# A block's opening: modulation columns in two channel halves, and the context loaded last

## Chip, cores and metric
The kernel runs on one core of one Trainium2 chip. The metric is device time in microseconds of one execution. Five engines work beside each other: TensorE (PE; PEld is its weight loads), VectorE (DVE), ScalarE (ACT), GpSimd (POOL) and SyncE (SP), which issues the loads. Each runs its own instructions in order and waits on semaphores.

## What is computed
Two stacked networks over 512 tokens of width 1024, in fp32. Only the start of the first matters here:

```python
mod_l = silu(c) @ w_mod + b_mod            # sh1, sc1, g1, sh2, sc2, g2: 6 parts of 1024
mod_c = silu(c_ctx) @ w_mod + b_mod        # the same for the context
pl = (rmsnorm(x, norm1_w) * (1 + sc1) + sh1) @ w_in         # 512 tokens
pc = (rmsnorm(ctx, norm1_w) * (1 + sc1c) + sh1c) @ w_in     # 256 context tokens
ml = mlstm(conv(pl), conv(pc)); hg = hgrn(pl, pc)           # then w_out, a convolved FFN, a second network
```

The opening needs sh1 and sc1 (2048 columns of w_mod) for c and c_ctx, the root of the mean square of each token, and the first slab of w_in.

## The kernel before
**Tiles.** x lies as 8 channel blocks (KD) of 128 channels by 512 tokens, the context cx as 8 by 256. A token tile is used as a sum of two fp32r parts: hh (high) and hl (low) for x, ch and cl for the context. Weights come in slabs of 256 columns (SLAB), all 8 channel blocks of them, and are split in the same way by GpSimd from raw into whi and wlo, in two buffers. A product is three matmuls: high by high, high by low, low by high. Slabs of w_in come in the order of IN1: slab 0 is "mq" (its output is then convolved), slab 1 "mv", slabs 2 and 3 the gates, slab 4 "mq" again.

**The opening** (first() on each engine). SP issues constants, x, cx, eight loads modraw[k] of 1024 KB (channel block k of w_mod, its first 2048 columns), then w_first (slab 0) into raw[0], all on one queue (L643 to L650). ACT squares x and then cx (L1040), DVE adds them up (L2052), PE sums over the partitions with a matrix of ones (square_sum, L3213), ACT takes the root by Ln and Exp (L1043, L1045), and DVE multiplies (L2058): xn for x, cx in place. PE makes the modulation (modulation, L2946): for each k four matmuls of 32 columns of silc (silu of c and c_ctx, the rest zero), by 512 columns of modraw[k], each into its own 32 partitions of pm[1][:, 0, :]. Group g holds columns 512g to 512g + 511, so 0 and 1 are sh1 and 2 and 3 are sc1. ACT copies the 128x512 result to modrow[0] (L1047); mod_turn (L2954) turns it into columns by four small products with the identity; DVE adds the bias and makes modc and wsc (L2064 to L2068), releasing mod_done. Matmuls of idle() (L3209) compute nothing that is used; they fill PE's waits.

**Tokens.** With wsc and modc ACT makes hh[k] (L1054) and for odd k a full-precision copy in pa[3] (L1058); DVE makes that copy for even k (L2078) and takes hl[k] as the difference (L2083). Both go through x's eight blocks and then the context's.

**Slabs.** Slab 0 is slab_opening: for each k six matmuls, as soon as the pieces of its weights (split_first on POOL, FIRST_PIECES) and hh[k], hl[k] are there. Slab 1 is slab_tok_late: clearing matmuls (L2864), then for four tiles of 128 tokens the products of whi (L2868), then those of wlo (L2872), then, once hl_done has counted all sixteen parts, the context's products (L2889 to L2891). Slab 0's result in pm[0] is read by ACT's centre copies (L1085) and by 16 tap operations of DVE (L1781), which then release pm_free[0]. On both engines they stand behind the context's parts. Slab 2 writes pm[0] again and waits for pm_free[0]; its first product is L2641. Loads of later slabs wait for splits, and splits for PE (slab_used).

Of the kernel before, what the change touches and what calls it, by code (L numbers as in the profile page):

```python
# [12 lines left out]
P = 128  # L13
# [37 lines left out]
MOD_GROUP = (0, 0, 0, 0, 1, 1, 2, 3)  # L51
# [24 lines left out]
DIAG_SLOT = (None, None, 8, 10)  # L76

# [95 lines left out]
def build(nc, io):  # L173
    with ExitStack() as ctx:
# [22 lines left out]
        modraw = [place(f"modraw{k}", [P, MOD_W], F32, arena + (12 + 4 * k) * TILE if k < 7 else raw_at - 8 * TILE) for k in range(KD)]  # L197
# [85 lines left out]
        def over_h(name, shape, n, dt=F32):  # L283
# [94 lines left out]
        mod_loaded, mod_used, mod_in, mod_done, lb_step, lb_exp = (  # L378
            [sem(f"mod_loaded{k}") for k in range(KD // 2)], sem("mod_used"), sem("mod_in"), sem("mod_done"), sem("lb_step"), sem("lb_exp"))
# [251 lines left out]
        def _(sp):  # L631
# [13 lines left out]
            sp.dma_start(cx[:].rearrange("p k t -> p (k t)"), io["ctxT"]).then_inc(ctx_loaded, 16)  # L645

            wm = io["w_mod"][0].rearrange("(k p) n -> k p n", p=P)
            for k in range(KD):
                sp.dma_start(modraw[k][:], wm[k][:, 0:MOD_W]).then_inc(mod_loaded[MOD_GROUP[k]], 16)
            sp.dma_start(raw[0][:].rearrange("p k n -> p (k n)"), io["w_first"]).then_inc(raw_loaded[0], 16)  # L650

            for i, (name, c0) in enumerate(IN1):
                if i == 0:
                    continue
                if i == 1:
                    sp.wait_ge(raw_loaded[0], 16)
                if i == 2:
# [353 lines left out]
        def _(act):  # L1011
            act.wait_ge(const_loaded, 16 * 2)
            act.wait_ge(const_made, 3)
            nc.scalar.activation(silc[:, :, 0:2], cols("c", 0, 16).rearrange("p (k j) -> p k j", j=2), ACT.Silu).then_inc(mod_in, 1)
# [17 lines left out]
            def first():  # L1032
                nc.scalar.preload_act_table_set("natural_log_exp_and_others")
                for n, (src, loaded, w) in enumerate(((x, x_loaded, T), (cx, ctx_loaded, CT))):
# [6 lines left out]
                for n, (acc, w) in enumerate(((std, T), (rstd, CT))):  # L1041
# [4 lines left out]
                act.wait_ge(mod_used, KD)  # L1046
                nc.scalar.activation(modrow[0][:], pm[1][:, 0, :], ACT.Copy).then_inc(mod_row, 1)  # L1047
                act.wait_ge(mod_done, 3)
                for n, (src, hi, w) in enumerate(((xn, hh, T), (cx, ch, CT))):
                    act.wait_ge(xn_done, KD * n + KD)  # L1050
                    if n:
                        act.wait_ge(hn_done, KD // 2)
                    for k in range(KD):
                        nc.scalar.activation(hi[:, k, :], src[:, k, :], ACT.Identity, bias=mod_col(0, k, n), scale=wsc[:, n, k:k + 1]).then_inc(hh_done, 1)  # L1054
                        if k % 2:
                            if KD * n + k >= 2:
                                act.wait_ge(hl_done, KD * n + k - 1)
                            nc.scalar.activation(pa[3][:, 0:w], src[:, k, :], ACT.Identity, bias=mod_col(0, k, n), scale=wsc[:, n, k:k + 1]).then_inc(xn_done, 1)  # L1058
# [677 lines left out]
        def _(v):  # L1736
# [306 lines left out]
            def first():  # L2043
                lower_bounds()

                for n, (acc, w) in enumerate(((std, T), (rstd, CT))):
# [8 lines left out]
                for n, (src, dst, w) in enumerate(((x, xn, T), (cx, cx, CT))):  # L2055
                    v.wait_ge(rstd_done, n + 1)
                    for k in range(KD):
                        nc.vector.tensor_tensor(dst[:, k, :], src[:, k, :], pa[n][:, 0:w], ALU.mult).then_inc(xn_done, 1)  # L2058

                v.wait_ge(mod_turned, 1)  # L2060
                to, bias = mod_turned_to(0)
                turned = mod_columns(pm[1][:, 1, :])
                raised = pm[1][:, 1, 4 * MOD_TILES1:5 * MOD_TILES1]
                nc.vector.tensor_tensor(raised.rearrange("p (j g t) -> p t g j", g=2, t=4), turned[:, :, 2:4, :], bias[:, :, 2:4, :], ALU.add).then_inc(mod_done, 1)  # L2064
                nc.vector.tensor_tensor(to[:, :, 0:2, :], turned[:, :, 0:2, :], bias[:, :, 0:2, :], ALU.add).then_inc(mod_done, 1)
                v.wait_ge(mod_done, 2)
                gain = cols("norm1", 0, KD).rearrange("p (o k) -> p o k", o=1).to_broadcast([P, 2, KD])
                nc.vector.scalar_tensor_tensor(wsc[:, 0:2, :], raised.rearrange("p (j k) -> p j k", j=2), 1.0, gain, ALU.add, ALU.mult).then_inc(mod_done, 1)  # L2068
                v.wait_ge(mod_done, 3)
                v.sem_inc(pm_free[1], 1)  # L2070
                for n, (src, hi, lo, w) in enumerate(((xn, hh, hl, T), (cx, ch, cl, CT))):
                    v.wait_ge(xn_done, KD * n + KD)
                    for k in range(KD):
# [6 lines left out]
                        else:  # L2080
                            v.wait_ge(xn_done, 2 * KD + KD // 2 * n + k // 2 + 1)
# [564 lines left out]
        def _(pe):  # L2646
            pe.wait_ge(const_loaded, 16 * 2)
            pe.wait_ge(const_made, 4)
# [29 lines left out]
            def slab_opening():  # L2678

                for k in range(KD):  # L2680
# [180 lines left out]
            def slab_tok_late(b, use, lo):  # L2861
# [32 lines left out]
            def in1(i, between=None):  # L2894
# [16 lines left out]
                elif name in ("mv", "hv"):  # L2911
                    if i == 1:
                        slab_tok_late(b, p, 2 + i + 1)
                    else:
                        slab_tok(b, p)
                    if between:
                        between()
                    pe.wait_ge(hl_done, 2 * KD)
                    last = context_tok(b, p)
                else:  # L2920
                    if i == 0:
                        last = slab_opening()
# [9 lines left out]
            def modulation(first_, end):  # L2932

                for i in range(first_, end):
                    k = i % KD
                    if i < KD:
                        pe.wait_ge(mod_loaded[MOD_GROUP[k]], 16 * MOD_GROUP.count(MOD_GROUP[k]))
                        src, out = modraw[k][:], pm[1][:, 0, :]
                    else:
                        b = mod_buffer(i)  # L2940
                        pe.wait_ge(mod_loaded[b], 16 * (MOD_GROUP.count(b) + sum(mod_buffer(j) == b for j in range(KD, i + 1))))
# [264 lines left out]
            def first():  # L3206
# [343 lines left out]
```

## Time and profile before

| | us |
|---|---|
| median of 3 runs (lowest, highest) | 3009.11 (3007.6, 3009.39) |
| the profiled execution | 3008.7 |
| its span in the trace | 3006.9 |
| PE busy | 2977.1 |
| POOL busy | 2075.4 |
| DVE busy | 1657.6 |
| ACT busy | 1048.0 |

The page gives for each engine the time in which it had an instruction under way. "Idle before" is time in which an engine waited, with the work that released it. Matmuls are pipelined, so the duration of one is longer than the distance of two that follow each other: 389 ns against 0.23 us for the common fp32r product of 512 columns. An fp32 matmul appears as two instructions, one for each pass. PEclk is the share of its full clock that was granted to PE. In the chain of waits and the timeline a row is start, length, and what ran; merged rows carry a count.

### The profile page before, as it was taken

Reading aid. Unit: us, or ns where it says so; the run is one execution under the profiler, and the core shown is the slowest. Engines: PE = TensorE matmul, PEld = TensorE weight load, DVE = VectorE, ACT = ScalarE, POOL = GpSimd, SP = SyncE. Lnnn points to the kernel's source line nnn. Section 1 sums busy time; section 2 is a strip of 40 time slices with the busy share of each in tenths; the row PEclk is TensorE's granted clock in tenths of the full one; section 3 lists DMA queues with packets and bytes.
Section 4 is the critical chain, followed back from the end, with each engine's and each line's share of the span. In section 5 each row is a group of like instructions: output and inputs, shape, how many; then the busy total and the mean of one; then the engine's idle time right before and its main releaser. Section 6 shows DMA issues by size and latency. Waiting matters only on the chain.

```text
span 3006.9 us, 49161 instructions
## 1 busy us (share of the span) xinstructions
PE 2977.1 (99%) x17179; PEld 2584.9 (86%) x17179; DVE 1657.6 (55%) x2214; ACT 1048.0 (35%) x1846; POOL 2075.4 (69%) x1583
## 2 busy tenths in 40 slices
PE   7999999999999999999999999999999999999999
PEld 5878978888889988887889998899888878899987
DVE  5753365889178742364347662577523652477631
ACT  4362153121146620232017650366301320166600
POOL 3614575888778887654777887788876546778874
PEclk9999999999999999999999999999999999999999
DMA  5202262322333333331223333333334313333332
GB/s 222 88 29 63 73 236 71 99 98 80 96 99 103 112 89 107 116 106 64 90 98 99 104 97 96 100 107 102 95 96 136 99 56 98 98 99 98 107 90 83
DMA packets 323100, 300.60 MB, mean 100 GB/s; under 512 B 6652, under 2 KB 316924, under 8 KB 319264
## 3 DMA queue, kind: packets, MB, share of 16 engines
q1 hardware_dynamic: 319056, 290.55, 30.5%
q10 hardware_dynamic: 3920, 8.36, 1.0%
q8 instruction: 82, 1.34, 0.2%
q14 instruction: 42, 0.34, 0.0%
HBM read 292.60 MB, written 2.10 MB: 98 GB/s over the span
## 4 chain that ended last, share of the span: by engine, by line
PE 96%; DVE 1%; DMA 1%; ACT 1%; issue 1%; SPq 0%; DVEq 0%; ACTq 0%
PE pm L2641 16%; PE pm L2643 16%; PE pm L2642 16%; PE pm L2770 8%; PE pm L2771 8%; PE pm L2772 8%; PE pa L2641 2%; PE pa L2643 2%; PE pa L2642 2%; PE pm L2720 1%; PE pm L2721 1%; PE pm L2722 1%; PE pm L3041 1%; DMA modraw<-in_w_mod 1%; PE pm L2671 1%; PE pa L3084 1%
## 5 line engine op out<-in xcount | busy, mean ns | idle before, releaser
L776 POOL TENSOR_TENSOR wlo<-raw,whi 128x512 fp32r<-128x512 f32 (+1 forms) x784 | 977.2, 1278 | 16.4
L772 POOL TENSOR_SCALAR whi<-raw 128x2048 fp32r<-128x2048 f32 (+1 forms) x196 | 336.5, 1717 | 699.8 <-PE pm L2643 326.5
L2641 PE MATMUL pm<-hh,whi 128*128 128x512 f32 x1064 | 421.2, 396 | 2.2 <-DVE sil L2408 2.2
L2643 PE MATMUL pm<-hh,wlo 128*128 128x512 f32 x1064 | 414.3, 389 | 0.0
L2642 PE MATMUL pm<-hl,whi 128*128 128x512 f32 x1064 | 414.3, 389 | 0.0
L794 POOL TENSOR_TENSOR wlo<-raw,whi 128x512 fp32r<-128x512 f32 x216 | 288.2, 1335 | 58.6 <-ACT whi L1445 41.1
L2770 PE MATMUL pm<-tsets,whi 128*128 128x256 f32 x1152 | 326.0, 283 | 0.0
L2771 PE MATMUL pm<-tsets,whi 128*128 128x256 f32 x1152 | 326.0, 283 | 0.0
L2772 PE MATMUL pm<-tsets,wlo 128*128 128x256 f32 x1152 | 326.0, 283 | 0.0
L2641 PE MATMUL pm<-uh,whi 128*128 128x512 f32 x836 | 325.4, 389 | 0.0
L2642 PE MATMUL pm<-ul,whi 128*128 128x512 f32 x836 | 325.2, 389 | 0.0
L2643 PE MATMUL pm<-uh,wlo 128*128 128x512 f32 x836 | 325.2, 389 | 0.0
L2770 PE MATMUL pm<-hh,whi 128*128 128x256 f32 x864 | 244.8, 283 | 0.1
L2771 PE MATMUL pm<-hl,whi 128*128 128x256 f32 x864 | 244.5, 283 | 0.0
L2772 PE MATMUL pm<-hh,wlo 128*128 128x256 f32 x864 | 244.5, 283 | 0.0
L2641 PEld LDWEIGHTS pm<-hh,whi 128*128 128x128 f32 x1064 | 199.8, 188 | 46.8 <-issue 5.7
L2642 PEld LDWEIGHTS pm<-hl,whi 128*128 128x128 f32 x1064 | 199.8, 188 | 43.7 <-issue 3.1
L2643 PEld LDWEIGHTS pm<-hh,wlo 128*128 128x128 f32 x1064 | 199.7, 188 | 42.0
L2356 DVE SCALAR_TENSOR_TENSOR x<-pm,x 128x512 f32 (+1 forms) x32 | 22.1, 692 | 374.4 <-PE pm L2643 374.4
L2770 PEld LDWEIGHTS pm<-tsets,whi 128*128 128x128 f32 x1152 | 221.2, 192 | 0.0
L2771 PEld LDWEIGHTS pm<-tsets,whi 128*128 128x128 f32 x1152 | 221.2, 192 | 0.0
L2772 PEld LDWEIGHTS pm<-tsets,wlo 128*128 128x128 f32 x1152 | 221.2, 192 | 0.0
(549 smaller groups left out, 6755.0 us busy)
## 6 DMA issues: line engine op xcount, KB each, us to landing
raw<-in_w_ffn SPq DMA_DIRECT2D x88, 1024.0 KB, 5.3
raw<-in_w_in SPq DMA_DIRECT2D x61, 1024.0 KB, 5.1
raw<-in_w_ffn SPq DMA_DIRECT2D x64, 704.0 KB, 4.6
raw<-in_w_up SPq DMA_DIRECT2D x22, 1024.0 KB, 5.1
raw<-in_w_out SPq DMA_DIRECT2D x12, 1024.0 KB, 5.1
raw<-in_w_down SPq DMA_DIRECT2D x16, 704.0 KB, 4.6
modbuf<-in_w_mod SPq DMA_DIRECT2D x10, 1024.0 KB, 5.6
modraw<-in_w_mod SPq DMA_DIRECT2D x8, 1024.0 KB, 19.7
```

Of the source, the lines that this page charges most:

```text
L772: nc.gpsimd.tensor_scalar(h, r, 1.0, 1.0, ALU.mult, ALU.mult).then_inc(hi_done, 1)
L776: last = nc.gpsimd.tensor_tensor(o[:, c], r[:, c], h[:, c].bitcast(F32), ALU.subtract)
L794: nc.gpsimd.tensor_tensor(operand(wlo, o), src, operand(whi, o).bitcast(F32), ALU.subtract).then_inc(st_pool, 1)
L2641: nc.tensor.matmul(out, wh, ah, start=start, stop=False)
L2642: nc.tensor.matmul(out, wh, al, start=False, stop=False)
L2643: return nc.tensor.matmul(out, wl, ah, start=False, stop=stop)
L2671: nc.tensor.matmul(pm[use][:, i, :], whi[b][:, k, P * i:P * i + P], src[:, k, :], start=k == 0 and src is hh, stop=False)
L2720: nc.tensor.matmul(o, hh[:, k, c], whi[b][:, k, :], start=k == 0, stop=False)
L2721: nc.tensor.matmul(o, hl[:, k, c], whi[b][:, k, :], start=False, stop=False)
L2770: nc.tensor.matmul(out, wh[:, k, :], th, start=start and k == 0, stop=False, skip_group_check=True)
L2771: nc.tensor.matmul(out, wh[:, k, :], tl, start=False, stop=False, skip_group_check=True)
L2772: last = nc.tensor.matmul(out, wl[:, k, :], th, start=False, stop=k == KD // 2 - 1, skip_group_check=True)
```

## The change
- **Two channel halves.** Each modraw[k] is loaded by two transfers of 512 KB: first the columns of channels 0 to 511 of sh1 and sc1 (groups 0 and 2), for all k, then those of channels 512 to 1023 (groups 1 and 3). PE makes the first half (modulation_half), ACT copies it as two blocks of 32 rows, half_turn turns it, DVE makes four of the eight columns of modc and wsc, and ACT and DVE make hh and hl of k 0 to 3. PE runs slab 0 for these k, then the second half's products, its turn, and slab 0 for k 4 to 7. modrow[0] is cleared at the start, since each turn reads all its rows.
- **w_first in two loads**, channel blocks 0 to 3 ahead of the last two pieces of the first half, and 4 to 7 behind the second half. split_first waits for each.
- **The context last.** cx is loaded behind all of these. Its squares, root, normalization and parts follow x's parts on ACT and DVE; its square_sum is a hook in slab 1, after the second of four token tiles.
- SP no longer waits for w_first before it issues slab 1. modraw[7] lies over whi[1] instead of in hl. full_made takes over one use of xn_done.

```diff
-MOD_GROUP = (0, 0, 0, 0, 1, 1, 2, 3)
+MOD_GROUP = (0, 0, 0, 0, 0, 0, 1, 1, 2, 2, 2, 2, 2, 2, 3, 3)
+FIRST_GROUP, FIRST_K = 1, 4
...
@@ SP @@
+            def mod_columns_of(half, k):
+
+                for_half = [a.rearrange("p (e h c) -> p h e c", e=2, h=2)[:, half] for a in (modraw[k][:], wm[k][:, 0:MOD_W])]
+                sp.dma_start(*for_half).then_inc(mod_loaded[MOD_GROUP[KD * half + k]], 16)
+
+            first_w = raw[0][:].rearrange("p k n -> p (k n)")
+            for k in range(KD):
+                if k == KD - 2:
+                    sp.dma_start(first_w[:, 0:FIRST_K * SLAB], io["w_first"][:, 0:FIRST_K * SLAB]).then_inc(mod_loaded[FIRST_GROUP], 16)
+                mod_columns_of(0, k)
+            for k in range(KD):
+                mod_columns_of(1, k)
+            sp.dma_start(first_w[:, FIRST_K * SLAB:], io["w_first"][:, FIRST_K * SLAB:]).then_inc(raw_loaded[0], 16)
             sp.dma_start(cx[:].rearrange("p k t -> p (k t)"), io["ctxT"]).then_inc(ctx_loaded, 16)
-
-            wm = io["w_mod"][0].rearrange("(k p) n -> k p n", p=P)
-            for k in range(KD):
-                sp.dma_start(modraw[k][:], wm[k][:, 0:MOD_W]).then_inc(mod_loaded[MOD_GROUP[k]], 16)
-            sp.dma_start(raw[0][:].rearrange("p k n -> p (k n)"), io["w_first"]).then_inc(raw_loaded[0], 16)
...
-                if i == 1:
-                    sp.wait_ge(raw_loaded[0], 16)
...
@@ POOL @@
+            nc.gpsimd.memset(modrow[0][:], 0.0).then_inc(const_made, 1)
...
-                pool.wait_ge(raw_loaded[0], 16)
+                pool.wait_ge(mod_loaded[FIRST_GROUP], mod_arrivals(FIRST_GROUP))
                 for i, (k0, k1) in enumerate(FIRST_PIECES):
+                    if k0 == FIRST_K:
+                        pool.wait_ge(raw_loaded[0], 16)
...
@@ ACT @@
+                squares(0)
+                roots(0)
+                act.wait_ge(mod_step, 2)
+                for g in (0, 2):
+                    rows = slice(32 * g, 32 * g + 32)
+                    nc.scalar.activation(modrow[0][rows, :], pm[1][rows, 0, :], ACT.Copy).then_inc(mod_step, 1)
+                act.wait_ge(mod_done, 3)
+                highs(0, 0, FIRST_K)
+                act.wait_ge(mod_used, KD)
+                for g in (1, 3):
+                    rows = slice(32 * g, 32 * g + 32)
+                    nc.scalar.activation(modrow[0][rows, :], pm[1][rows, 0, :], ACT.Copy).then_inc(mod_step if g == 1 else mod_row, 1)
+                act.wait_ge(mod_done, 6)
+                highs(0, FIRST_K, KD)
+                squares(1)
+                roots(1)
+                act.wait_ge(hn_done, KD // 2)
+                highs(1, 0, KD)
...
@@ DVE @@
+                square_sums(0)
+                normalized(0, 0, FIRST_K)
+                v.wait_ge(mod_step, 5)
+                mod_columns_made(0)
+                lows(0, 0, FIRST_K)
+                normalized(0, FIRST_K, KD)
+                v.wait_ge(mod_turned, 1)
+                mod_columns_made(1)
+                v.sem_inc(pm_free[1], 1)
+                lows(0, FIRST_K, KD)
+                square_sums(1)
+                normalized(1, 0, KD)
+                lows(1, 0, KD)
                 v.sem_inc(hn_done, KD)
                 mlstm()
...
@@ PE @@
+                    if between and t == 1:
+                        between()
...
-                    for g in range(4):
+                    for g in range(4) if i >= KD else (1, 3):
                         last = nc.tensor.matmul(out[32 * g:32 * g + 32, :], silc[:, k, :], src[:, T * g:T * g + T], start=k == 0, stop=k == KD - 1)
...
+            def modulation_half():
+
+                for k in range(KD):
+                    pe.wait_ge(mod_loaded[MOD_GROUP[k]], mod_arrivals(MOD_GROUP[k]))
+                    for g in (0, 2):
+                        last = nc.tensor.matmul(pm[1][32 * g:32 * g + 32, 0, :], silc[:, k, :], modraw[k][:, T * g:T * g + T], start=k == 0, stop=k == KD - 1)
+                last.then_inc(mod_step, 1)
+
+            def half_turn(half, bank, done):
+
+                which = ident[:].rearrange("p (g c) -> p g c", g=4)[:, half::2, 0:2]
+                for t in range(4):
+                    last = nc.tensor.matmul(bank[:, 8 * t:8 * t + 8].rearrange("p (g j) -> p g j", g=4)[:, half::2, :], modrow[0][:, P * t:P * t + P], which, start=True, stop=True)
+                last.then_inc(done, 1)
...
                 square_sum(0, std, T)
                 idle(8)
-                pe.wait_ge(mod_in, 1)
-                for k, _ in enumerate(modulation(0, KD)):
-                    if k == 3:
-                        square_sum(1, rstd, CT)
-                    if k == 6:
-                        idle(4)
+                pe.wait_ge(mod_step, 1)
+                modulation_half()
+                idle(4)
+                pe.wait_ge(mod_step, 4)
+                half_turn(0, pm[1][:, 1, :], mod_step)
+                idle(5)
+                slab_opening(0, FIRST_K)
+                for _ in modulation(0, KD):
+                    pass
+                pe.wait_ge(mod_step, 6)
                 pe.wait_ge(mod_row, 1)
-                mod_turn(modrow[0], pm[1][:, 1, :])
-                idle(5)
+                half_turn(1, pm[1][:, 1, :], mod_turned)
                 for i in range(4):
-                    in1(i)
+                    in1(i, (lambda: square_sum(1, rstd, CT)) if i == 1 else None)
```

## Rows read from the trace of the kernel before

**Rows 1.** The page, busy time of the engines.
```profile
PE 2977.1 (99%) x17179; PEld 2584.9 (86%) x17179; DVE 1657.6 (55%) x2214; ACT 1048.0 (35%) x1846; POOL 2075.4 (69%) x1583
```

**Rows 2.** Waits of PE, whole run: us in total, times, longest.
```profile
PE pa L3213 <- DVE std L2052: 18.1, 1, 18.1
PE pm L2641 <- DVE sil L2408: 2.2, 2, 1.1
```

**Rows 3.** The chain that ended last, in the opening: start, us, what.
```profile
34.79 0.61 ACT modrow L1047
...
37.99 1.19 PE pm L2685 x2
```

**Rows 4.** Timeline of PE, opening: start, us, instruction [idle before <-releaser].
```profile
19.93 3.62 PE L3209 MATMUL pm<-ident 128*128 128x128 f32 x16
...
27.58 0.70 PE L3213 MATMUL pa<-rstd,ones 128*128 128x256 f32 x2
...
33.66 1.07 PE L2946 MATMUL pm<-modraw,silc 128*32 128x512 f32 x8 [0.33 <-DMA modraw<-in_w_mod]
```

**Rows 5.** Timeline of PE, slab 1 and the start of slab 2.
```profile
51.21 0.38 PE L2868 MATMUL pm<-whi,hh 128*128 128x256 f32 x1
...
62.81 0.28 PE L2889 MATMUL pa<-whi,ch 128*128 128x256 f32 x1
...
68.57 0.40 PE L2641 MATMUL pm<-hh,whi 128*128 128x512 f32 x1
```

**Rows 6.** Timeline of DVE, opening and slabs 0 and 1.
```profile
18.26 3.60 DVE L2052 TENSOR_TENSOR rstd<-rstd,sq 128x256 f32<-128x256 f32 x7
...
29.24 2.74 DVE L2058 TENSOR_TENSOR cx<-cx,pa 128x256 f32<-128x256 f32 x8 [2.60 <-ACT pa L1045]
...
40.71 1.36 DVE L2083 TENSOR_TENSOR hl<-pa,hh 128x512 fp32r<-128x512 f32 x2
...
46.22 0.54 DVE L2078 TENSOR_SCALAR pa<-cx,wsc,modc 128x256 f32<-128x256 f32 x1
...
52.15 9.73 DVE L1781 SCALAR_TENSOR_TENSOR cacc<-pm,col,cacc 128x441 f32<-128x441 f32 x16 [0.19 <-ACT cacc L1085]
```

**Rows 7.** Windows: PE, PEld, DVE, ACT, POOL busy; PEclk, DMA share, GB/s.
```profile
12.00:23.70 11.70, 5.46 (x18) 4.17 (x18) 10.24 (x20) 8.05 (x17) 0.00 (x0) 1.00 1.01 428
23.70:33.70 10.00, 8.60 (x70) 2.93 (x73) 5.68 (x13) 0.86 (x2) 0.00 (x0) 1.00 1.01 418
37.90:41.30 3.40, 3.31 (x8) 2.69 (x9) 2.77 (x5) 3.40 (x6) 3.23 (x5) 0.50 1.01 338
41.30:50.70 9.40, 9.40 (x43) 7.47 (x42) 8.97 (x18) 9.40 (x18) 8.95 (x9) 1.00 0.11 30
78.00:3006.00 2928.00, 2919.78 (x16824) 2539.68 (x16822) 1616.66 (x2130) 1013.00 (x1788) 2049.81 (x1546) 1.00 0.31 97
```

**Rows 8.** Timeline of all engines: SP's issues of w_mod, ACT's first squares.
```profile
2.63 6.89 SPq L649 DMA_DIRECT2D modraw<-in_w_mod  x8
...
11.28 4.27 ACT L1040 ACTIVATE sq<-x 128x512 f32<-128x512 f32 x8 [4.34 <-DMA x<-in_xT]
```

**Rows 9.** fp32 products of 512 columns (ns, min/median/max), and two modulation weight loads.
```profile
L2946 PE MATMUL pm<-modraw,silc x64: 592/592/826, 23.8 to 34.1; 128*32 128x512 f32 x64
...
L2988 PE MATMUL pa<-mq,mk x48: 590/592/697, 157.3 to 222.7; 128*128 128x512 f32 x48
...
24.46 0.14 PEld L2946 LDWEIGHTS pm<-modraw,silc 128*32 128x32 f32 x4 [0.45 <-issue]
24.89 0.14 PEld L2946 LDWEIGHTS pm<-modraw,silc 128*32 128x32 f32 x4 [0.29 <-issue]
```

**Rows 10.** Timeline of PE, slab 0's third channel block and slab 1's first matmul.
```profile
42.40 0.62 PE L2685 MATMUL pm<-hh,whi 128*128 128x512 f32 x2
...
50.67 0.60 PE L2864 MATMUL pm<-zrow 1*128 1x512 bf16 x2
```

**Rows 11.** Loads by kind: count, size, median us from issue to landing.
```profile
raw<-in_w_gate SPq DMA_DIRECT2D x2, 256.0 KB, 2.7
```

More of the change, by code:

```diff
@@ L196, in build @@
         TILE = 4 * T
-        modraw = [place(f"modraw{k}", [P, MOD_W], F32, arena + (12 + 4 * k) * TILE if k < 7 else raw_at - 8 * TILE) for k in range(KD)]
+        modraw = [place(f"modraw{k}", [P, MOD_W], F32, arena + (12 + 4 * k) * TILE if k < 7 else raw_at + 12 * TILE) for k in range(KD)]
         uh = place("uh", [P, KF, T], F32R)
@@ L377, in build @@
         mod_row, mod_turned = sem("mod_row"), sem("mod_turned")
-        mod_loaded, mod_used, mod_in, mod_done, lb_step, lb_exp = (
-            [sem(f"mod_loaded{k}") for k in range(KD // 2)], sem("mod_used"), sem("mod_in"), sem("mod_done"), sem("lb_step"), sem("lb_exp"))
+        full_made = sem("full_made")
+        mod_loaded, mod_used, mod_step, mod_done, lb_step, lb_exp = (
+            [sem(f"mod_loaded{k}") for k in range(KD // 2)], sem("mod_used"), sem("mod_step"), sem("mod_done"), sem("lb_step"), sem("lb_exp"))
         ctx_free = [sem("ctx_free0"), sem("ctx_free1")]
@@ L1033, in first, with squares @@
                 nc.scalar.preload_act_table_set("natural_log_exp_and_others")
-                for n, (src, loaded, w) in enumerate(((x, x_loaded, T), (cx, ctx_loaded, CT))):
+                def squares(n):
+                    src, loaded, w = ((x, x_loaded, T), (cx, ctx_loaded, CT))[n]
                     act.wait_ge(loaded, 16)
@@ L1040, in first, with roots @@
                         nc.scalar.activation(sqs[m % 4][:, 0:w], src[:, k, :], ACT.Square).then_inc(sq_done, 1)
-                for n, (acc, w) in enumerate(((std, T), (rstd, CT))):
+                def roots(n):
+                    acc, w = ((std, T), (rstd, CT))[n]
                     act.wait_ge(sq_summed, n + 1)
@@ L1045, in first, with highs @@
                     nc.scalar.activation(pa[n][:, 0:w], acc[:, 0:w], ACT.Exp, scale=-0.5).then_inc(rstd_done, 1)
[L1046 to L1053, printed above, removed]
+                def highs(n, k0, k1):
+                    src, hi, w = ((xn, hh, T), (cx, ch, CT))[n]
+                    for k in range(k0, k1):
+                        act.wait_ge(xn_done, KD * n + k + 1)
                         nc.scalar.activation(hi[:, k, :], src[:, k, :], ACT.Identity, bias=mod_col(0, k, n), scale=wsc[:, n, k:k + 1]).then_inc(hh_done, 1)
@@ L2044, in first, with square_sums @@
                 lower_bounds()
-                for n, (acc, w) in enumerate(((std, T), (rstd, CT))):
+                def square_sums(n):
+                    acc, w = ((std, T), (rstd, CT))[n]
                     for k in range(KD):
@@ L2054, in first, with normalized @@
                             nc.vector.tensor_copy(acc[:, 0:w], sqs[m % 4][:, 0:w]).then_inc(sq_added, 1)
-                for n, (src, dst, w) in enumerate(((x, xn, T), (cx, cx, CT))):
+                def normalized(n, k0, k1):
+                    src, dst, w = ((x, xn, T), (cx, cx, CT))[n]
                     v.wait_ge(rstd_done, n + 1)
-                    for k in range(KD):
+                    for k in range(k0, k1):
                         nc.vector.tensor_tensor(dst[:, k, :], src[:, k, :], pa[n][:, 0:w], ALU.mult).then_inc(xn_done, 1)
-                v.wait_ge(mod_turned, 1)
@@ L2067, in first, with mod_columns_made @@
[L2067 to L2073, printed above, removed]
+                def mod_columns_made(half):
+                    to, bias = mod_turned_to(0)
+                    turned = mod_columns(pm[1][:, 1, :])
+                    raised = pm[1][:, 1, 4 * MOD_TILES1:5 * MOD_TILES1]
+                    at, scaled, ks = slice(half, half + 1), slice(2 + half, 3 + half), slice(FIRST_K * half, FIRST_K * half + FIRST_K)
+                    nc.vector.tensor_tensor(raised.rearrange("p (j g t) -> p t g j", g=2, t=4)[:, :, at, :], turned[:, :, scaled, :], bias[:, :, scaled, :], ALU.add).then_inc(mod_done, 1)
+                    nc.vector.tensor_tensor(to[:, :, at, :], turned[:, :, at, :], bias[:, :, at, :], ALU.add).then_inc(mod_done, 1)
+                    v.wait_ge(mod_done, 3 * half + 2)
+                    gain = cols("norm1", 0, KD).rearrange("p (o k) -> p o k", o=1)[:, :, ks].to_broadcast([P, 2, FIRST_K])
+                    nc.vector.scalar_tensor_tensor(wsc[:, 0:2, ks], raised.rearrange("p (j k) -> p j k", j=2)[:, :, ks], 1.0, gain, ALU.add, ALU.mult).then_inc(mod_done, 1)
+                    v.wait_ge(mod_done, 3 * half + 3)
@@ L2074, in first, with lows @@
+                def lows(n, k0, k1):
+                    src, hi, lo, w = ((xn, hh, hl, T), (cx, ch, cl, CT))[n]
+                    v.wait_ge(xn_done, KD * n + k1)
+                    for k in range(k0, k1):
                         full = pa[2 + k % 2][:, 0:w]
@@ L2676, in slab_first, with slab_opening @@
                 return last
-            def slab_opening():
-                for k in range(KD):
+            def slab_opening(a, b):
+                for k in range(a, b):
                     piece = [k0 <= k < k1 for k0, k1 in FIRST_PIECES].index(True)
@@ L2859, in slab_late, with slab_tok_late @@
                 return last
-            def slab_tok_late(b, use, lo):
+            def slab_tok_late(b, use, lo, between=None):
                 for a in range(2):
@@ L2912, in in1 @@
                     if i == 1:
[L2913 removed]
+                        slab_tok_late(b, p, 2 + i + 1, between)
                     else:
                         slab_tok(b, p)
[L2916 to L2917 removed]
+                        if between:
+                            between()
                     pe.wait_ge(hl_done, 2 * KD)
@@ L2921, in in1 @@
                     if i == 0:
-                        last = slab_opening()
+                        last = slab_opening(FIRST_K, KD)
                     elif i == GATE_AT + 2:
@@ L2940, in modulation @@
                         b = mod_buffer(i)
-                        pe.wait_ge(mod_loaded[b], 16 * (MOD_GROUP.count(b) + sum(mod_buffer(j) == b for j in range(KD, i + 1))))
+                        pe.wait_ge(mod_loaded[b], mod_arrivals(b) + 16 * sum(mod_buffer(j) == b for j in range(KD, i + 1)))
                         src, out = modbuf[b], pm[0][:, 1, :]
```

21 lines of the change are left out of this document (9 added, 12 removed).

## The prediction

> **What bounds the kernel now.** I read the page's engine table first: TensorE (PE) is busy 99% of the span, GpSimd (POOL) 69%, the rest less [rows 1]. Then who makes PE wait, over the whole run: almost all of it lies in the opening. The reader is to see that 18.1 us pass before the first sum of squares, and that behind the opening no wait is over 1.1 us [rows 2]. So whatever moves the moment at which PE gets through its first slabs moves the end by as much, unless something later waits for another engine. The chain of waits ends the opening with one ACT copy, the turn, the DVE columns, the first high half of the tokens, and the first slab product at 37.99 [rows 3]. PE's timeline has what it does before: fillers and products behind the loads, the last of which it gets at 33.66 [rows 4]. Last, I read how much slack two chains beside PE have in slab 1: the context, and the convolution that frees the accumulator of slab 0 [rows 5, 6].
>
> **Loads.** The engines move 428 GB/s, 2.45 us per 1024 KB [rows 7]; x lands at 11.28, where its squares begin [rows 8]. After x come now 512 KB pieces, 1.23 us each: six halves by 18.7, the first half of slab 0's weights and the other two halves by 22.4, the second channel half by 32.2, the rest of slab 0 by 33.5, the context by 35.9. Shorter runs may be slower: slab weights with 1 KB runs moved at 338 GB/s, the transfer's ramps included [rows 7]; the pieces have runs of 2 KB. By that end the first half is in at 26.8 and the second at 39. PE reaches each of them later either way (below), so they cost nothing; it would bind under some 300 GB/s. SyncE issued eight loads in 6.89 us [rows 8]; sixteen take 13.8, ahead of the transfers.
>
> **The modulation twice.** A 128x512 fp32 product lasts 592 ns at 32 columns as at 128, and the weight loads of four column groups come every 0.43 us [rows 9]: four groups run beside each other, one pass takes 0.43 us, and an fp32 product has two passes. With two groups I expect the same pass, so a half costs 8 x 2 x 0.43 = 6.9 us. Bounds: 3.4 us if the passes of one group could overlap too, 13.8 if the two groups did not; the rows of both widths are nearest to 6.9. The eight steps were there before, but behind the loads: only 1.07 us of them came after the last one [rows 4]. Now neither half is hidden. The first begins at 23.6, when the 16 fillers end [rows 4]; it costs 6.9, 0.23 for first products of 826 ns, and 0.17 of tail (592 ns less one pass): it ends at 30.9.
> **The chain to the slab** took 37.99 - 34.73 = 3.26 us from the last product's end [rows 3, 4]. The copy of the row, 0.60 us, becomes two copies of 32 rows and the same 512 columns, one behind the other: 0.55 more (nothing if the rows counted, 0.6 at most). DVE's three small operations are as many as before in each half. First slab product at 30.9 + 3.8 = 34.7, **3.3 us earlier** than before. The four fillers after the products and the five after the turn stay inside this stretch. GpSimd's added memset stands in the first microseconds, ahead of constants and x, which land later; it splits the first pieces from 22.4 on: both nothing.
> **Slab 0 is cut in two.** Its pace is (50.67 - 42.40) / 6 = 1.38 us for one of eight channel blocks [rows 10]; PE waited for nothing in it but 0.3 us for the first high part, so ACT and DVE keep up. Four blocks: 5.5, to 40.2. Then PE does the second half: 16 passes and tail, 7.0, to 47.2, and again the chain of 3.8 us, in which it has only the turn to do, to 51.0. Four blocks: 56.5. Before, slab 0 ended at 50.67.
> **Clock.** Before, PE's granted clock was 0.50 (1.2 GHz) from 37.9 to 41.3 and 1.00 (2.4 GHz) around it [rows 7]: the engine had spent the 3.3 us before it on waits, the turn and small fillers. That made slab 0 12.68 us long instead of 8 x 1.38 = 11.0: 1.7 us. I take one such stretch after each of the two gaps, as the first is like the old one and the second emptier: 3.4 us, slab 0 ends at 59.9, 9.2 us later than before. With none it is 5.8 later, with one 7.5.
> The Trainium skill (TensorE: Matmul & The Clock Gate, the table on why this matters for kernels) warns against idle gaps between bursts of products, and so against a plan that adds gaps. By it the longer wait found below would bring a third slow stretch; the trace of before has the one drop only, after a gap that held fillers.
>
> **The context.** Its squares were taken beside the loads, and its high and low parts made from 46.22 to 51.96, while PE was in slab 0. Now all of it starts when slab 0's tokens are done, and the sum of squares is a product in slab 1, after the second of four token tiles. Slab 1: 0.54 us to clear, 11.60 for the latent products (the high ones, two thirds, first), 5.76 for the context, 17.9 in all [rows 5, 10]. The sum stands at 0.54 + 3.9 = 4.4 us into slab 1. The squares are done by then: the fourth low part was made 4.1 us after the first slab product [rows 6], so DVE is free 4.1 us into the second part of slab 0 with 1.4 to go, and its adds took 4.0 us [rows 6]: they end 1.8 us before the sum. From that product to the end of the normalization it was 31.98 - 27.58 = 4.4 us, and the parts take 5.7 more [rows 4, 6]: ready at 14.6. PE stands before the context products at 4.4 + 0.5 (the sum itself) + 7.8 = 12.7: **it waits 1.9 us**.
> **The convolution.** ACT's centre copies and DVE's sixteen taps of slab 0 come after the context in program order on both engines. They read pm[0], and slab 2 (gate) waits for it (pm_free). Before: taps from 52.15 to 61.88, slab 2 at 68.57, slack 6.7 us [rows 5, 6]. Now they begin 52.15 - 46.22 = 5.9 us after the parts do, at 14.8 into slab 1, take 9.73 and end at 24.5. PE ends slab 1 at 14.6 + 5.76 = 20.3, so **it waits 4.2 us more**. Slab 1 to slab 2: 24.6 instead of 17.9, 6.7 lost.
>
> **Sum:** slab 2 begins 9.2 + 6.7 = 15.9 us later. The later loads, splits and waits hang on PE's slabs by semaphores and shift with it. The profiled execution took 3008.7 (span 3006.9 and 1.8 around it), 0.4 under the median of the three runs: 3008.7 + 15.9 = **3024.6**, 0.5% slower. A measurement of this kernel tells 0.2%, 6 us, from no change.
>
> **Rivals.**
> - *Clock.* One slow stretch less gives 3022.9, none 3021.2; one more, after the wait of 4.2 us, 3026.3. These are the forecast's own range, 3020.5 to 3028. Beyond it: two column groups may not hold the clock, which four held with PE busy 8.6 of 10 us [rows 7]. Each half at 1.2 GHz costs 6.9 more: 3031.5 for one. 0.10.
> - *Cheap halves.* If a half costs 3.4 us, 2 x 3.45 comes off: 3017.7. For it: a pass of two groups is in no row. Against: rows 9. 0.06.
> - *A shorter context chain.* If DVE and ACT were through with the context and the taps earlier, the 6.2 us of waits go: 3018.4. It needs the chain of 24.5 us to be under 18.4; its parts are measured, and it starts only at PE's sum. 0.06.
> - *Loads one by one.* A load of 256 KB lands 2.7 us after its issue [rows 11]; if pieces did not overlap, nine would end at 11.28 + 24.3 = 35.6 and eighteen at 59.9, some 12 us later than PE wants them: 3037. Against it: eight loads were queued at once and the engines moved 418 to 428 GB/s throughout [rows 7]. 0.02. The Trainium skill (DMA: Bandwidth & Descriptors, rules for kernel authors) asks for at least 1 MiB per DMA for full bandwidth, which speaks for this rival.
> - *Faster.* The opening was bound by the loads, and the first product does come 3.3 us earlier. If PE would have waited in slab 0 anyway, the second half and its chain fit into those waits and the gain stays: 3005.4. It decides from 7.0 + 3.8 = 10.8 us of waits in slabs 0 and 1, context included; the rows show 0.3. 0.04.
> - *No difference at the end,* as a later stage waits for another engine and swallows the delay: 3009. PE is idle 8.2 of the 2928 us after 78 [rows 7]. 0.04.
>
> **How the numbers follow.** The forecast has 0.68. From 3017 to 3029 lie it, the cheap halves and the shorter chain: 0.80. Faster by over 0.2%: 0.04, and 0.01 for what I don't see: 0.05; within 0.2%: 0.04; slower: 0.91.
>
> **What would show it.** In the changed profile: the first product of slab 0 near 34.7; products of the second half from 40 to 42 on, seven us long with passes of 0.43; behind them a gap of over 3 us with only the turn in it; slab 0's end at 57 to 60; a PE wait of about 2 us for the context's low parts, and one of about 4 us for DVE's taps before the gate slab, which begins at 81 to 85; one to three stretches of clock 0.50. The prediction is wrong if a half takes 3.4 us, if PE finds pm[0] free, or if the distance from slab 2 to the end is not what it was.

## The result

The changed kernel takes 3025.13 us (median of 5 executions, 3023.66 to 3025.78) against 3009.11 for the kernel before (3007.6 to 3009.52): ratio 1.0055, 95% interval 1.0043 to 1.0066. The profiled execution has a span of 3022.3 us, before it was 3006.9.

The page after, busy time of the engines (before: rows 1). PE has 7.5 us more, the others what they had:

```profile
PE 2984.6 (99%) x17187; PEld 2586.7 (86%) x17187; DVE 1657.4 (55%) x2217; ACT 1049.6 (35%) x1849; POOL 2075.8 (69%) x1584
```

Waits of PE after, whole run (us in total, times, longest). Of these only the first and the 2.2 us for sil were there at this length before [rows 2]; the new ones are 4.1 for the taps (named by DVE's queue), 1.5 for the context's low parts, and 1.5 and 1.4 in the second chain:

```profile
PE pa L3296 <- DVE std L2097: 18.5, 1, 18.5
PE pm L2707 <- DVEq L1825: 4.1, 1, 4.1
PE pm L2707 <- DVE sil L2474: 2.2, 2, 1.1
PE pm L2751 <- ACT hh L1077: 1.7, 2, 1.5
PE pa L2957 <- DVE cl L2135: 1.5, 1, 1.5
PE pm L3030 <- ACT modrow L1094: 1.4, 1, 1.4
```

Timeline of PE after, the opening (start, us, instruction, idle before). It answers to rows 3, 4 and 10: fillers, first half's products, turn, slab 0, second half's products, turn, slab 0's second part, slab 1.

```profile
20.35 2.44 PE L3292 MATMUL pm<-ident 128*128 128x128 f32 x16
22.71 7.06 PE L3023 MATMUL pm<-modraw,silc 128*32 128x512 f32 x32
29.71 1.16 PE L3292 MATMUL pm<-ident 128*128 128x128 f32 x8
31.07 1.05 PE L3030 MATMUL pm<-ident,modrow 128*128 128x4 f32 x8 [0.21 <-ACT modrow L1088]
31.99 1.36 PE L3292 MATMUL pm<-ident 128*128 128x128 f32 x10
33.60 0.69 PE L2751 MATMUL pm<-hh,whi 128*128 128x512 f32 x2 [0.25 <-ACT hh L1077]
...
39.25 7.06 PE L3014 MATMUL pm<-modraw,silc 128*32 128x512 f32 x32
47.71 1.03 PE L3030 MATMUL pm<-ident,modrow 128*128 128x4 f32 x8 [1.39 <-ACT modrow L1094]
...
50.20 1.19 PE L2751 MATMUL pm<-hh,whi 128*128 128x512 f32 x2 [1.47 <-ACT hh L1077]
...
58.34 0.60 PE L2930 MATMUL pm<-zrow 1*128 1x512 bf16 x2
```

Further on, the first context product of slab 1 and the first product of slab 2 (before: rows 5, without a wait):

```profile
72.54 0.39 PE L2957 MATMUL pa<-whi,ch 128*128 128x256 f32 x1 [1.48 <-DVE cl L2135]
...
82.60 0.59 PE L2707 MATMUL pm<-hh,whi 128*128 128x512 f32 x1 [4.05 <-DVEq L1825]
```

DVE after (before: rows 6): squares' adds, context normalized, its parts, then the taps, which end at 82.40:

```profile
54.58 3.60 DVE L2097 TENSOR_TENSOR rstd<-rstd,sq 128x256 f32<-128x256 f32 x7
64.36 2.73 DVE L2106 TENSOR_TENSOR cx<-cx,pa 128x256 f32<-128x256 f32 x8 [6.18 <-ACT pa L1070]
67.14 0.55 DVE L2130 TENSOR_SCALAR pa<-cx,wsc,modc 128x256 f32<-128x256 f32 x1
...
72.67 9.73 DVE L1823 SCALAR_TENSOR_TENSOR cacc<-pm,col,cacc 128x441 f32<-128x441 f32 x16 [0.19 <-ACT cacc L1127]
```

Windows after, columns as in rows 7: the first two around the two stretches of half clock, the third with the loads of the first half.

```profile
48.67:55.50 6.83, 5.36 (x14) 4.17 (x14) 5.70 (x12) 6.21 (x12) 4.86 (x4) 0.50 0.11 36
82.90:86.30 3.40, 3.40 (x9) 2.65 (x8) 0.00 (x0) 0.68 (x2) 0.00 (x0) 0.51 0.86 295
...
24.00:31.00 7.00, 6.87 (x36) 2.37 (x32) 0.42 (x1) 1.15 (x2) 3.96 (x6) 1.00 1.05 387
```

**Where the time went.** Slab 2 begins at 82.60 instead of 68.57, 14.0 us later; what follows takes 2939.7 instead of 2938.3, 1.4 us more. Together 15.4, the difference of the spans. The 1.4 us go with the second stretch of half clock, which is 3.4 us long and would cost half of that, 1.7; they are not a sharp number, since the runs below that have no such stretch before or in slab 2 differ in this by 1.2 us (2937.9 to 2939.1).

### The profile page after: what moved, and what is told of

Its sections match the earlier page's. It is cut to its first block, busy times and chain, and to the rows that moved or that the text cites. A ratio compares the mean times of both kernels' runs of the same rounds, so it can differ in the third digit from the quotient of the medians.

```text
span 3022.3 us, 49197 instructions
## 1 busy us (share of the span) xinstructions
PE 2984.6 (99%) x17187; PEld 2586.7 (86%) x17187; DVE 1657.4 (55%) x2217; ACT 1049.6 (35%) x1849; POOL 2075.8 (69%) x1584
## 4 chain that ended last, share of the span: by engine, by line
PE 96%; DVE 2%; ACT 1%; issue 1%; DMA 0%; DVEq 0%; SPq 0%; ACTq 0%
PE pm L2707 16%; PE pm L2709 16%; PE pm L2708 16%; PE pm L2836 8%; PE pm L2837 8%; PE pm L2838 8%; PE pa L2707 2%; PE pa L2709 2%; PE pa L2708 2%; PE pm L2786 1%; PE pm L2787 1%; PE pm L2788 1%; PE pm L3124 1%; PE pm L2737 1%; PE pa L3167 1%; PE pm L2741 1%
## 5 line engine op out<-in xcount | busy, mean ns | idle before, releaser
L2708 PEld LDWEIGHTS pm<-hl,whi 128*128 128x128 f32 x1064 | 200.1, 188 | 43.7 <-issue 3.1
```

The lines of the kernel that those rows point to most:

```text
L2708: nc.tensor.matmul(out, wh, al, start=False, stop=False)
```

## The experiments

All in the table are timed beside the kernel before in the same rounds, whose median was 3009.11 for the changed kernel, 3007.99 for the next four, 3007.72 for the four after them, and 3007.6 for between_r. "Less before" is the median less that one; medians of different rounds are not to be compared directly. The next columns have what each trace shows in us: slab 0's first product, the distance from it to slab 2's first product, the span less the latter's start, and the lengths of the stretches with a granted clock of 0.50 up to slab 2.

| kernel | median | less before | ratio (95% interval) | slab 0 | slab 0 to 2 | rest | half clock |
|---|---|---|---|---|---|---|---|
| before | 3009.11 | | | 37.99 | 30.6 | 2938.3 | 3.4 |
| changed | 3025.13 | 16.0 | 1.0055 (1.0043 to 1.0066) | 33.60 | 49.0 | 2939.7 | 6.8, 3.4 |
| ctx_early | 3017.04 | 9.0 | 1.0028 (1.0017 to 1.0039) | 34.05 | 41.7 | 2937.9 | 3.4 |
| ctx_late | 3014.15 | 6.2 | 1.0021 (1.0012 to 1.0031) | 35.30 | 36.7 | 2940.1 | 3.4 |
| no_taps | 3018.94 | 10.9 | 1.0033 (1.0021 to 1.0046) | 34.98 | 43.7 | 2938.7 | 3.4 |
| fill_both | 3020.61 | 12.6 | 1.0040 (1.0026 to 1.0054) | 33.84 | 46.5 | 2938.2 | none |
| one_step | 3019.27 | 11.5 | 1.0037 (1.0023 to 1.0051) | 34.30 | 43.0 | 2939.7 | 6.8, 3.4 |
| sum_first | 3019.18 | 11.5 | 1.0036 (1.0022 to 1.0050) | 34.39 | 45.0 | 2938.1 | 3.4, 3.4 |
| before_fill | 3007.60 | -0.1 | 0.9998 (0.9988 to 1.0008) | 38.41 | 29.0 | 2938.4 | none |
| between | 3008.55 | 0.8 | 1.0002 (0.9992 to 1.0011) | 35.83 | 32.5 | 2939.1 | none |
| between_r | 3005.97 | -1.6 | 0.9993 (0.9984 to 1.0002) | 35.27 | 30.0 | 2938.9 | none |

The stretch of half clock after the second turn is not the same in the five traces that have it: of slab 0's products 5.3 us ran in it in the changed kernel, 5.5 in one_step, 3.4 in ctx_early, 3.1 in sum_first and 2.9 in no_taps, so it cost from 1.5 to 2.7 us. Two distances can differ by 1.2 us for that alone.

### The two parts, each alone

**ctx_early** keeps the halves and puts the context back beside the loads:

```diff
             sp.dma_start(x[:]..., io["xT"]).then_inc(x_loaded, 16)
+            sp.dma_start(cx[:]..., io["ctxT"]).then_inc(ctx_loaded, 16)
...
                 squares(0)
+                squares(1)
                 roots(0)
+                roots(1)
...
                 highs(0, FIRST_K, KD)
-                squares(1)
-                roots(1)
```

with the same moves on DVE, and the sum on PE after the first half's fourth step.

> The change with its context part undone: the context is loaded behind x again, squared, summed and normalized beside the loads; the two channel halves stay. My theory (the halves cost PE a second 7 us of products and a second chain of 3.9 us; the context costs 6.4 us of PE waits in slab 1 and a stretch of half clock behind them): PE finds the context's parts and the accumulator ready, slab 1 to slab 2 takes 17.9 us instead of 24.3, the half-clock stretch at 83 goes, 0.5 us for the sum of squares comes into the first half: 3025.1 - 6.4 - 1.7 + 0.5 = 3017.5. Rival A (all the cost is in the halves): 3025. Rival B (all is in the context's lateness): 3009.

Measured: 3017.04. Of PE's waits in slabs 1 and 2 nothing is left; slab 1's first matmul is at 57.88 and slab 2's first product at 75.78, 17.9 us later:

```profile
57.88 0.60 PE L2929 MATMUL pm<-zrow 1*128 1x512 bf16 x2
...
75.78 0.40 PE L2706 MATMUL pm<-hh,whi 128*128 128x512 f32 x1
```

Both rivals fall. The halves alone cost 0.28%.

**ctx_late** is the kernel before with one modulation, and the context's load, squares and sum where the change has them.

> The other part alone: the kernel before, one modulation of four groups, but the context loaded last and its sum taken in the middle of slab 1. My theory: the loads of w_mod end 2.5 us earlier and with them slab 0 begins at 35.5 instead of 38.0; slab 1 to slab 2 takes 24.3 us instead of 17.9; a half-clock stretch of 1.7 us comes behind the wait: 3009.1 - 2.5 + 6.4 + 1.7 = 3014.7, 3013.0 without the stretch. Rival A (all the cost is in the halves): 3006.6. Rival B (all in the context): 3025.

Measured: 3014.15. The loads do give their 2.5 us (slab 0 at 35.30 instead of 37.99), and the context's chain takes more than that back:

```profile
PE pm L2668 <- DVEq L1796: 4.0, 1, 4.0
...
PE pa L2918 <- DVE cl L2092: 1.5, 1, 1.5
PE pa L3242 <- DVE rstd L2067: 1.1, 1, 1.1
```

The 1.1 us for the squares' sum is new and no theory had it; pool_held below is about it. The two parts cost 9.0 and 6.2 us in their rounds, together 15.2, against the change's 16.0. They are not quite additive: ctx_late has the load gain that the halves give in another way, and each has a stretch of half clock.

### The steps of the sum

**one_step** leaves out seven of the eight steps of the second half:

```diff
+                    if 0 < i < KD:
+                        pe.sem_inc(mod_used, 1)
+                        yield
+                        continue
                     for g in range(4) if i >= KD else (1, 3):
```

> The changed kernel with one of the eight channel steps of the second modulation half: the products of the other seven are left out (the values of channels 512 to 1023 of shift and scale are then wrong). My theory (the second half is on PE's own path, 0.86 us for a step of two groups, its loads and copies long done or unchanged): 3025.1 - 7 x 0.86 = 3019.1. Rival (PE would wait there anyway, for loads, for normalized tokens or for the rest of slab 0's weights): 3023 to 3025.

Measured: 3019.27. The second half's products shrink from 7.06 to 1.05 us, and the distance from slab 0 to slab 2 by the same 6.0; the waits behind it are the same 1.4, 1.5, 1.5 and 4.0. (Less before, the median gives 4.5 us, 11.5 instead of 16.0: in this trace 0.7 us are lost ahead of slab 0, whose start is 34.30 instead of 33.60.)

```profile
39.91 1.05 PE L3018 MATMUL pm<-modraw,silc 128*32 128x512 f32 x4
42.36 1.02 PE L3034 MATMUL pm<-ident,modrow 128*128 128x4 f32 x8 [1.40 <-ACT modrow L1094]
```

So nothing hid the second half, and a step of two groups costs 0.86 us, as a step of four does.

**no_taps** takes the convolution off DVE:

```diff
-                conv(0)
+                for e in range(2):
+                    v.wait_ge(ml_centre, e + 1)
+                v.sem_inc(conv_step, 16)
+                v.sem_inc(pm_free[IN1_P[0]], 1)
```

> The changed kernel, but DVE leaves out the sixteen taps of slab 0's convolution (9.7 us; the convolved values are then wrong) and frees pm[0] when ACT's centre copies are done. My theory (slab 2 waits for these taps and for nothing else): PE's wait of 4.05 us before slab 2 goes, and the half-clock stretch behind it: 3025.1 - 4.1 - 1.7 = 3019.3; 3021.0 if the clock drops in any case. Rival (something else, such as the gate slab's weights, is due at the same time): 3025.

Measured: 3018.94. PE no longer waits before slab 2, and the clock stays up there; the distance falls by 5.3 us, 4.05 of it the wait, most of the rest the shorter stretch of half clock in slab 0:

```profile
PE pa L2960 <- DVE cl L2138: 1.5, 1, 1.5
...
78.60:82.00 3.40, 3.40 (x20) 2.91 (x19) 0.00 (x0) 3.12 (x4) 2.34 (x5) 1.00 0.00 0
```

**sum_first** moves the sum of squares alone:

```diff
-                    in1(i, (lambda: square_sum(1, rstd, CT)) if i == 1 else None)
+                    if i == 1:
+                        square_sum(1, rstd, CT)
+                    in1(i)
```

> The changed kernel with the context's sum of squares ahead of slab 1 instead of behind its second token tile, 4.4 us sooner; nothing else. My theory (the context's chain starts at this product, and the convolution of slab 0 hangs on its end): PE's wait for the context's low parts goes, that for the taps falls from 4.1 to 1.7 us, slab 2 begins 4.1 us sooner, and with the shorter wait the half-clock stretch goes: 3025.1 - 4.1 - 1.7 = 3019.3; 3021.0 if the clock still drops. Rival (DVE or ACT are busy with other work until then, so the place of the sum does not matter): 3025.

Measured: 3019.18. Slab 0 to slab 2 takes 45.0 us instead of 49.0, as expected, and the rest is 1.6 us shorter. PE finds the low parts and pm[0] ready; DVE's taps begin at 69.28 and end at 79.01, slab 2 begins at 79.34:

```profile
69.28 3.03 DVE L1823 SCALAR_TENSOR_TENSOR cacc<-pm,col,cacc 128x441 f32<-128x441 f32 x5 [0.18 <-ACT cacc L1127]
```

The total came out for reasons that the expectation did not have. It left 1.7 us of wait for the taps, and there is none; in their place PE waits 1.1 us for the squares ahead of the sum, and a new stretch of half clock of 3.4 us falls into slab 1:

```profile
59.31 0.70 PE L3296 MATMUL pa<-rstd,ones 128*128 128x256 f32 x2 [1.13 <-DVE rstd L2097]
...
60.93:64.34 3.41, 3.41 (x19) 3.41 (x18) 3.29 (x10) 2.58 (x6) 0.00 (x0) 0.50 0.67 205
```

The place of this one product, chosen inside slab 1, carried some 5 of the change's 16 us: 4.5 by the medians less before, 5.6 by the trace from slab 0 on.

### The clock

**fill_both** adds unused products, five before and five behind the second turn, fourteen before slab 2:

```diff
+                fill(5, pa[1])
                 pe.wait_ge(mod_step, 6)
                 pe.wait_ge(mod_row, 1)
                 half_turn(1, pm[1][:, 1, :], mod_turned)
+                fill(5, pa[1])
...
                     in1(i, (lambda: square_sum(1, rstd, CT)) if i == 1 else None)
+                    if i == 1:
+                        fill(14, pa[0])
```

> The changed kernel with unused small products where PE waits: five before and five behind the second turn (gap 46.3 to 50.2), fourteen before slab 2 (gap 78.5 to 82.6). My theory of the clock (it falls because PE is nearly idle there: 5.3 us of slab 0 and 3.4 us of slab 2 ran at 1.2 GHz, half of which is lost): both stretches go and the waits stay: 3025.1 - 2.6 - 1.7 = 3020.8. Rival (the fillers are too small to count, or only take time): 3025 to 3026.

Measured: 3020.61, 12.6 us over the kernel before instead of 16.0. The fillers take the place of idle time in the same gaps, and the granted clock is 1.00 (2.4 GHz) through both stretches in which it was 0.50 (1.2 GHz) in the changed kernel:

```profile
48.00:56.00 8.00, 7.75 (x42) 6.39 (x42) 5.89 (x13) 6.44 (x13) 5.68 (x5) 1.00 0.12 34
80.00:86.00 6.00, 5.65 (x30) 4.93 (x31) 0.15 (x1) 1.15 (x2) 1.02 (x1) 1.00 0.55 174
```

**before_fill** does this in the kernel before: three more fillers ahead of the turn, one more behind it.

> The kernel before with three more unused products ahead of the turn and one more behind it. My theory of the clock: the half-clock stretch at 37.9 to 41.3 goes, 1.7 us less where it occurs, 3007.4 against 3009.1, within what these rounds can tell. Rival (it comes whatever PE does): 3009.1.

Measured: 3007.60 against 3007.72, which tells nothing of the total. The trace has slab 0 to slab 2 in 29.0 us instead of 30.6 and no half clock, as expected. But ctx_late and pool_held, whose gap is that of the kernel before without added fillers, have none there either (in before and in these two PE is busy 2.3 of its 3.3 us), so one trace does not show that the fillers did it.

### A version meant to beat both

**between** keeps one modulation and loads the context late, but takes DVE's adds out of its chain. ACT squares two channel blocks at a time between the pairs of high parts, and PE adds the squares up inside slab 0. It has the fillers of before_fill, and w_first in two loads with the context's between them:

```diff
+                highs(0, 0, 2)
+                act.wait_ge(ctx_loaded, 16)
+                context_square(0)
+                highs(0, 2, 4)
+                context_square(1)
+                highs(0, 4, 6)
+                context_square(2)
+                context_square(3)
+                highs(0, 6, KD)
...
+                    for j in range(4):
+                        for e in range(2):
+                            last = nc.tensor.matmul(pa[1][:, 0:CT], ones[:], sqs[j][:, CT * e:CT * e + CT], start=j + e == 0, stop=j + e == 4)
```

> A version meant to beat both: one modulation of four groups as in the kernel before; the context loaded behind w_mod and the first half of slab 0's weights; ACT squares it in four operations between the pairs of high parts, PE adds the squares itself (eight products after the sixth channel block of slab 0, 1.8 us instead of 0.5), so that DVE's and ACT's context parts come at the old distance; fillers as in the run before_fill. My theory (w_mod's loads bound the opening, and lateness of the context costs only what reaches slab 2): loads 2.5 us earlier, 1.3 us more on PE, no wait in slabs 1 and 2, no half-clock stretch: slab 2 at 65.6 instead of 68.6, 3009.1 - 2.9 = 3006.2. Rival (any late context delays the taps past slab 2): 3010 to 3014.

Measured: 3008.55, no gain. Slab 2 is free of waits as expected, but it begins at 68.28 instead of 65.6: I had reckoned an fp32 pass of 256 columns at 0.11 us, and the sixteen take 0.23 each:

```profile
44.10 3.61 PE L3267 MATMUL pa<-sq,ones 128*128 128x256 f32 x16
```

**between_r** has squares and ones as fp32r, for which the trace has one pass instead of two, of about half the length (1.13 us for eight):

> The run between with one thing changed: in it the eight products that add the context's squares took 3.61 us for sixteen fp32 passes of 256 columns (0.23 each, where I had reckoned 0.11) and ate the gain of the earlier loads. Here squares and ones are fp32r, one pass each, at the 0.12 us that the context's products of 256 columns show: 0.95 us, 2.7 less. Slab 2 at 65.6 instead of 68.28: 3005.9 against 3007.7 for the kernel before of those rounds, 1.8 us faster (0.06%, at the edge of what five rounds tell). Rival (the squares' operations on ACT and the later context hold slab 0 or slab 1 up once PE is quicker): 3007.5 to 3008.5.

Measured: 3005.97 against 3007.6, ratio 0.9993, interval 0.9984 to 1.0002. The trace agrees to 0.4 us, slab 2 at 65.25:

```profile
43.55 1.13 PE L3271 MATMUL pa<-sqr,ones_r 128*128 128x256 f32 x8
...
47.35 0.60 PE L2916 MATMUL pm<-zrow 1*128 1x512 bf16 x2
```

Its span is 3004.1 against 3006.9. It beats the changed kernel beyond doubt; that it beats the kernel before is likely and not shown, since the interval holds 1.

### DVE's adds beside GpSimd

**pool_held** is ctx_late with one wait more:

```diff
                     pool.wait_ge(mod_used, KD)
+                    pool.wait_ge(sq_added, 2 * KD)
```

> The run ctx_late with GpSimd's split of slab 1 held until DVE has added up the context's squares. In ctx_late these adds took 1321 ns each (median) while GpSimd split, 425 ns in the kernel before and in the changed kernel, where GpSimd was idle. Theory (the two engines hold each other up in SBUF): the seven adds fall to 0.43 us each, all done by 47.5 instead of 52.0; the split starts then, and PE waits for slab 1's high part until about 49.4, so no gain in time is expected. Rival (the adds are slow for another reason, such as products or loads beside them): they stay above 1 us.

In ctx_late the view of the adds' line has (ns, min/median/max) the first row; in pool_held the seven adds are back at 3.60 us together, and GpSimd splits after them:

```profile
L2067 DVE TENSOR_TENSOR rstd<-rstd,sq x7: 489/1321/1403, 44.4 to 51.6; 128x256 f32<-128x256 f32 x7
```

```profile
44.19 3.60 DVE L2068 TENSOR_TENSOR rstd<-rstd,sq 128x256 f32<-128x256 f32 x7
...
48.11 1.90 POOL L771 TENSOR_SCALAR whi<-raw 128x2048 fp32r<-128x2048 f32 x1
```

The rival falls: in the changed kernel the same adds took 425 ns each with products beside them all the time and the DMA engines busier than in ctx_late (a share of 0.21 against 0.16), and GpSimd idle. As expected there is no gain in time, and rather a loss, since PE waits 3.3 us for slab 1's high part (3019.06, a single execution).

## Why the prediction was right, and where it was lucky

The forecast was 3024.6; 3025.13 was measured. In the profiled executions, on which its sum rests, slab 2 and the end come 15.4 us later where it had 15.9. Step by step:

- **The modulation twice: right.** A half of two groups takes 7.06 us; 7.3 and 7.0 were forecast. The trace of the changed kernel and one_step leave no room for a half of 3.4 us.
- **The chain to the slab: right.** 3.83 and 3.89 us against 3.8. The two copies of 32 rows take 1.20 us, 0.60 each like the one copy of 128 rows before [rows 3], so the rows saved nothing here.
- **The context and the convolution: right, a little long.** Slab 1 to slab 2 takes 24.26 us against 24.6; the waits are 1.48 and 4.05 against 1.9 and 4.2. no_taps, sum_first and ctx_early each confirm one link.
- **Loads: right that they don't bind.** The 512 KB pieces with runs of 2 KB moved at 387 to 391 GB/s, between the 428 and the 338 that bounded them. (The bound's times were a piece too long: at 338 GB/s the halves are in at 25.2 and 37.7, not 26.8 and 39; nothing hangs on it.) The rule of the Trainium skill (DMA: Bandwidth & Descriptors, Rules for kernel authors) that asked for 1 MiB per DMA agrees with these 9%, without effect on the time. But the length of the run has a part in them, as loads of one size show: in the trace a packet of 2 KB took 86 to 88 ns, one of 4 KB, of w_first's pieces of 512 KB, 164 to 167, and one of 8 KB of the context 314. The load's size alone was not varied.
- **The start of the first half: 0.9 us early,** 22.71 instead of 23.6: the sixteen passes of the fillers took 2.44 us instead of 3.62, and began 0.4 later. In the other runs they took 2.51 to 3.56. They follow 0.21 us apart up to 21.4 and 0.11 apart from there on; in the kernel before they are 0.21 apart to the end. The trace's record of the granted clock begins, with 1.00, at 21.4 and at 24.3 in the two, and PEclk in the windows reads 1.00 ahead of it only because nothing is recorded there. So the moment at which the clock comes up varies from run to run. It was treated as fixed and is not.
- **The clock: right in sum, wrong in place.** I put one stretch of 1.7 us after each gap. After the first there was none (PEclk 1.00 from 31 to 47). That gap of 3.8 us was no shorter than the old one, but not "like" it: all nine fillers lie in it and PE was busy 3.4 of 3.8 us, where the old gap had five of them and 2.3 of 3.3 us (the other four stood ahead of the last product). After the second it was 0.50 from 48.7 to 55.5, and 5.3 us of products ran at half speed, 2.6 us lost. A third came after the wait for the taps, 1.4 us, which had been given to a rival. Forecast 3.4, measured 4.0. The step that failed is "I take one such stretch after each of the two gaps", with the 1.7 us for each: in the traces the first gap, with its fillers, never dropped the clock in six kernels with two halves, and the second, without, did in all five that left it so, and did not in fill_both. The third stretch, behind 4.05 us of idle time, is the one that the warning of the Trainium skill (TensorE: Matmul & The Clock Gate, Why this matters for your kernels) had named, and the trace agrees with it there. The second came behind two idle times of 1.4 and 1.5 us with the turn between them, each well under the gap that the table gives. Why the old gap dropped the clock in the trace of before, but not in ctx_late and pool_held with the very same contents, stays open: the same gap can go either way.

So the terms erred by -0.9 (fillers), -1.7 (first stretch), +0.9 (second), +1.4 (third), -0.3 (slab 1) and +0.1 (all others), in sum by -0.5 us in the profiled executions; the medians are 16.0 apart, 0.5 more than the forecast gave them (15.5). The range was earned by the mechanisms, the closeness in part by errors of both signs.

**Why the change lost.** Before, eight steps of modulation ran inside the wait for the loads and cost PE 1 us. The change starts slab 0 4.4 us sooner and pays with 7.1 us of products that nothing covers, 3.9 us of chain, 1.1 us more in slab 0's own products (half clock for the most part), and 6.4 us from slab 1 to slab 2: 5.5 of waits for a context that before had been ready in time and for the taps behind it, and 0.8 for the sum of squares, which now stands in slab 1, and for what products lose at either side of a wait. That is 14.0; 1.4 more come after it. The slack that it spent was seen ahead: 6.7 us between DVE's taps and slab 2 [rows 5, 6].

## What to carry to other kernels

Work that lies behind loads is free only as long as it stays there: before you cut such a step in two to start sooner, see whether a half costs half (here two column groups cost as much as four) and what covers the second one. When a side branch is moved later, follow it to its last customer, here taps that free an accumulator, and compare its length with the slack there; then place its first operation on the busy engine as early as its input allows, since 4.4 us of place were worth 4.5 us of time or a little more. In gaps of PE that can't be closed, fillers were worth 3.4 us (12.6 over the kernel before instead of 16.0).

## What the hardware showed unexpectedly

- A DVE add of two SBUF tiles of 128x256 fp32 took 425 ns with GpSimd idle and 1321 ns (median) beside GpSimd's split of a slab, also in SBUF; the split's four steps took 5.59 us instead of 5.0. pool_held separates the two and the adds return to their old length; in the changed kernel they have it too, with products beside them throughout.
- The clock fell 1.5 us before the products that suffered, in the idle gap itself, and was down for 6.8 us behind a gap with only the turn in it; in three other kernels with the very same gap it was down for 3.4 us, as in the kernel before [rows 7].
